# A conv FFN's down product, six of eight tiles by Strassen's scheme, with VectorE making the weight sums

## The reference, cut to what matters

```python
def conv_ffn(x, w_up, conv_w, conv_b, w_down):
    u = causal_depthwise_conv(x @ w_up.astype(x.dtype), conv_w, conv_b)
    g, val = jnp.split(u, [FFN_DIM_2], axis=-1)
    return (jax.nn.gelu(g) * val) @ w_down.astype(x.dtype)
...
        h = h + conv_ffn(rms_norm_2(h, ffn_norm[layer]), ffn_w_up[layer], ffn_conv_w[layer],
                         ffn_conv_b[layer], ffn_w_down[layer])
```

## Time and profile before

| | |
|---|---|
| time, median of 3 runs | 2938.76 us |
| span of the profiled execution, first to last instruction | 2937.1 us |
| mean granted clock of the tensor engine | 0.999 |
| busy: PE, VectorE (DVE), ScalarE (ACT), POOL | 99%, 45%, 44%, 45% |
| up product of the first conv FFN | about 2000 to 2262.6 us |
| down product of the first conv FFN | 2262.6 to 2393.1 us |

### The profile page before, as it was taken

One profiled execution on the slowest core, in us unless ns is written; L12 is line 12 of the kernel. 1 busy time (PEld: TensorE's weight loads), 2 busy tenths in 40 slices (PEclk: granted clock), 3 DMA queues, 4 the chain that ended last, 5 costly groups with the idle time before them and its releaser, 6 DMA issues.

```text
span 2937.1 us, 40238 instructions
## 1 busy us (share of the span) xinstructions
PE 2919.6 (99%) x14312; PEld 2388.5 (81%) x14312; DVE 1309.0 (45%) x2190; ACT 1288.6 (44%) x2017; POOL 1322.3 (45%) x743
## 2 busy tenths in 40 slices
PE   9999999999999999999999999999999999999999
PEld 7888888888878888888888877778888887888887
DVE  5657534221063667434222076654554138455510
ACT  4556545322253556444223265554444228444421
POOL 4454355444434554455444443444444443444443
PEclk9999999999999999999999999999999999999999
DMA  4222232323322232333333322212333322233333
GB/s 145 73 87 80 81 122 92 99 94 100 108 86 87 73 98 68 94 115 106 94 99 101 108 80 71 61 56 94 98 95 98 95 94 94 93 100 93 100 104 90
DMA packets 77275, 273.37 MB, mean 93 GB/s; under 512 B 8776, under 2 KB 9416, under 8 KB 77152
## 3 DMA queue, kind: packets, MB, share of 16 engines
q1 hardware_dynamic: 74112, 266.05, 29.0%
q10 hardware_dynamic: 3040, 5.64, 0.6%
HBM read 269.55 MB, written 2.10 MB: 92 GB/s over the span
## 4 chain that ended last, share of the span: by engine, by line
PE 93%; DVE 2%; ACT 2%; POOL 1%; issue 1%; DMA 0%; SPq 0%; DVEq 0%; ACTq 0%; POOLq 0%
PE ps L822 25%; PE ps L824 25%; PE ps L823 25%; PE ps L1122 2%; PE ps L1153 2%; PE ps L1100 2%; PE ps L1375 2%; PE ps L1381 1%; PE ps L1376 1%; PE ps L1226 1%; PE ps L1232 1%; PE ps L1227 1%; ACT WHI L1534 1%; PE ps L1095 1%; PE ps L1097 0%
## 5 line engine op out<-in xcount | busy, mean ns | idle before, releaser
L2894 POOL TENSOR_TENSOR WLO<-WRAW,WHI 128x1024 fp32r<-128x1024 f32 x393 | 949.8, 2419 | 1158.5 <-ACT WHI L1534 1158.2
L822 PE MATMUL ps<-HH,WHI 128*128 128x512 f32 x2144 | 842.1, 393 | 2.4 <-POOL WLO L2894 0.9
L824 PE MATMUL ps<-HH,WLO 128*128 128x512 f32 x2144 | 834.8, 389 | 0.0
L823 PE MATMUL ps<-HL,WHI 128*128 128x512 f32 x2144 | 834.4, 389 | 0.0
L1534 ACT ACTIVATE WHI<-WRAW 128x1024 fp32r<-128x1024 f32 x467 | 490.6, 1051 | 281.6 <-DMA WRAW<-wall 280.8
L822 PEld LDWEIGHTS ps<-HH,WHI 128*128 128x128 f32 x2144 | 402.5, 188 | 91.2 <-issue 5.3
L824 PEld LDWEIGHTS ps<-HH,WLO 128*128 128x128 f32 x2144 | 402.4, 188 | 84.7
L823 PEld LDWEIGHTS ps<-HL,WHI 128*128 128x128 f32 x2144 | 402.7, 188 | 81.1
L2746 DVE SCALAR_TENSOR_TENSOR ps<-U,COLS,ps 128x512 f32<-128x512 f32 x192 | 145.0, 755 | 122.6 <-ACT ps L1993 108.5
L2228 DVE TENSOR_TENSOR ACC<-ACC,SQ 128x512 f32<-128x512 f32 x78 | 68.4, 877 | 280.5 <-ACT SQ L1819 271.1
L2980 POOL TENSOR_SCALAR SG<-SG,RS 128x512 f32<-128x512 f32 (+3 forms) x104 | 109.9, 1067 | 141.1 <-DVE RS L2508 141.1
(11 more groups left out here) (422 smaller groups left out, 4805.4 us busy)
## 6 DMA issues: line engine op xcount, KB each, us to landing
WRAW<-wall SPq DMA_DIRECT2D x502, 512.0 KB, 3.5
y<-X ACTq DMA_DIRECT2D x8, 256.0 KB, 4.0
X<-xin SPq DMA_DIRECT2D x3, 512.0 KB, 7.9
DFT<-dft ACTq DMA_DIRECT2D x4, 258.0 KB, 4.3
PT_IN<-pin ACTq DMA_DIRECT2D x2, 512.0 KB, 3.7
DIL<-dil ACTq DMA_DIRECT2D x1, 768.0 KB, 4.6
X<-xin SPq DMA_DIRECT2D x2, 256.0 KB, 4.7
COLS<-cols ACTq DMA_DIRECT2D x1, 290.5 KB, 5.3
```

Of the source, the lines that this page charges most:

```text
L822: pe.matmul(out_, WHI[w_at], x_hi, start=first, stop=False)
L823: pe.matmul(out_, WHI[w_at], x_lo, start=False, stop=False)
L824: return pe.matmul(out_, WLO[w_at], x_hi, start=False, stop=last)
L2894: pool.tensor_tensor(WLO[:, s, :], whole, WHI[:, s, :].bitcast(F32), ALU.subtract).then_inc(wt_lo, 1)
```

## The change

The conv FFN is cut into three chunks. A chunk makes 4 rounds of the up product (8 row tiles), then a new stage `down` adds these 8 row tiles' share of all 8 output tiles to X. `down` has 8 units: a direct one (output tile 0, 8 row tiles, as before), six paired ones, and a direct one (output tile 7). Three pairs of output tiles (1 and 2, 3 and 4, 5 and 6) take two paired units each. A paired unit holds two pairs of row tiles for one pair of output tiles, that is, twice four weight blocks of 128 x 128. In place of 8 block products by 256 tokens each it makes 7, of mixed operands (`PRODUCTS`), each by three matmuls of 256 columns: 42 matmuls a unit.

What is new beside the products:
- **weight sums**: four sums of 256 columns a unit, of 2, 2, 3 and 3 blocks, made by VectorE with `tensor_reduce` (`sums_of`). They stand in VectorE's program three units ahead of use, in the up stage before the wait for the unit itself. ScalarE and POOL then split 768 kept columns and 1024 columns of sums (`split_paired`, `remainder_paired`).
- **operand mixes**: at the end of each up round VectorE makes four halves of mixed token columns in three operations (`mixed`), ScalarE copies their high parts, VectorE subtracts for the low.
- **recombination**: per pair ScalarE copies one product and VectorE takes seven operations to add the pair to X (`pair_added`).
- **order on PE**: the last row tile of the first direct unit comes after the first paired unit. The first and third pair use the four convolution banks. The direct tile's slot comes free with the first paired unit's.
- the rounds of both stages are written out; there is no loop. In the first layer's last chunk the work for the next norm follows each finished tile (`finished`).

Cut to its core:

```diff
+CHUNKS = ((0, 4), (4, 4), (8, 4))
+HALF = SEQ // 2
+EXTRA = 4
+A12, A11, A22, A21 = range(4)
+R1, R3, R2, R4 = range(4)
+KEPT = 3 * 2 * P
+PRODUCTS = ((0, "slot", A11, B11), (2, "slot", A12, B21), (1, "extra", R2, T2), (3, "extra", R4, B22),
+            (4, "slot", A22, T4), (5, "extra", R1, T1), (6, "extra", R3, T3))
...
+            def down(st):
+                weights(st.unit(0))
+                pe.wait_ge(bank_free[st.bank(0)], st.use(0))
+                direct(0, 0, range(kt - 1))
+                for j, p, b in paired_steps(st):
+                    if p == 1 and b == 0:
+                        pe.wait_ge(bank_free[st.bank(0)], st.use(4))
...
+                    if p == 2 and b == 0:
+                        pe.wait_ge(S["pair_step"], st.at("pair_step", PAIR_STEPS))
+                    weights(st.unit(j))
...
+                    for i in range(2):
+                        k = 2 * b + i
+                        if p == 0:
+                            pe.wait_ge(S["operand_ready"], up.at("operand_ready", 3, k))
+                        for h, home, block_, x in PRODUCTS:
+                            if p == 0 and k == 0 and h in (0, 4):
+                                pe.wait_ge(S["product_ready"], up.at("product_ready", 1 + h // 4, up.reps - 1))
...
+                            pe.matmul(o, w_hi, FTH[:, row, cols_], start=first, stop=False, skip_group_check=True)
+                            pe.matmul(o, w_hi, FTL[:, row, cols_], start=False, stop=False, skip_group_check=True)
+                            mm = pe.matmul(o, w_lo, FTH[:, row, cols_], start=False, stop=last, skip_group_check=True)
+                    if j == 1:
+                        direct(0, 0, range(kt - 1, kt)).then_inc(unit_used, 2)
+                    else:
+                        mm.then_inc(unit_used, 1)
...
+                direct(j, 3, range(kt)).then_inc(unit_used, 1)
...
+            def split_paired(n):
+                act.activation(WHI[:, s, 0:KEPT], WRAW[:, s, 0:KEPT], ACT.Copy).then_inc(slot_hi, 1)
+                act.wait_ge(*sums_ready(n))
+                act.activation(XHI[:, e, :], XRAW[:, e, :], ACT.Copy).then_inc(wt_hi, 1)
...
-                        t = r * 2 + j // 2
-                        c = t + (FT2 if j % 2 else 0)
+                        c = st.t + r * 2 + j // 2 + (FT2 if j % 2 else 0)
+                        sums_of(st, j, r)
                         dve.wait_ge(unit_used, st.unit(j, r) + 1)
                         scaled(st, j, r, U[:, j, 2:2 + SEQ])
...
-                            remainder(st, (tile_of(t, F2H), tile_of(t, F2L)), SG[:, j, :], 1 + j // 2, r)
-                repeat(dve, st, body)
+                            if j == 3:
+                                mixed(st, r, halves(SG), (2, 3, 6, 7))
+                            remainder(st, (FTH[:, 4 * r + j // 2, :], FTL[:, 4 * r + j // 2, :]), SG[:, j, :], 1 + j // 2, r)
+                    remainder(st, mixed_rows(r), TM[:, :, :], 3, r)
+                repeat(dve, st, body, st.reps)
+
+            def sums_of(st, j, r=0):
+                n = st.unit(j, r) + AHEAD
...
+                w = WRAW[:, s, :].rearrange("p (b c) -> p c b", c=2 * P)
+                dve.wait_ge(raw[s], 16 * (n // SLOTS + 1))
+                for i, blocks in ((R1, slice(A22, A21 + 1)), (R3, slice(A11, A21 + 1, 2)), (R2, slice(A11, A21 + 1)), (R4, slice(A12, A21 + 1))):
+                    dve.tensor_reduce(sum_of(e, i), w[:, :, blocks], AXX, ALU.add).then_inc(summed["vector"], 1)
+
+            def mixed(st, r, b, at):
+                dve.wait_ge(S["product_ready"], st.at("product_ready", 2, r))
+                dve.tensor_tensor(t[:, 0:2, :], b[:, b12:b12 + 1, :].to_broadcast([P, 2, HALF]), b[:, b11:b22 + 1:b22 - b11, :], ALU.subtract)\
+                   .then_inc(S["mixed"], 1)
+                dve.wait_ge(S["mixed"], st.at("mixed", 1, r))
+                dve.tensor_tensor(t[:, 2, :], t[:, 1, :], b[:, b11, :], ALU.subtract).then_inc(S["mixed"], 1)
+                dve.wait_ge(S["mixed"], st.at("mixed", 2, r))
+                dve.tensor_tensor(t[:, 3, :], b[:, b21, :], t[:, 2, :], ALU.add).then_inc(S["mixed"], 1)
...
+            def down(st):
+                for j in range(st.units):
+                    p = ended_at(st, j - 1)
+                    if j == 2:
+                        direct_added(st, 0, 0, 0)
+                    if p is not None:
+                        pair_added(st, p)
+                    sums_of(st, j)
+                    if st.last and j:
+                        for t in tiles_done(st, j - 1):
+                            finished(st, t)
+                direct_added(st, DT - 1, st.units - 1, 3)
...
+            def remainder_paired(n):
...
+                pool.wait_ge(*sums_ready(n))
+                pool.wait_ge(slot_hi, PAIRED[n] + 1)
+                pool.tensor_tensor(WLO[:, s, 0:KEPT], WRAW[:, s, 0:KEPT], WHI[:, s, 0:KEPT].bitcast(F32), ALU.subtract)
+                pool.wait_ge(wt_hi, n + 1)
+                pool.tensor_tensor(XLO[:, e, :], XRAW[:, e, :], XHI[:, e, :].bitcast(F32), ALU.subtract).then_inc(wt_lo, 1)
```

More of the change, by code:

```diff
@@ L124, with pair_order @@
 COL, N_COLS = column_plan()
+def pair_order(pairs, blocks):
+    return [None] + [(p, b) for p in range(pairs) for b in range(blocks)] + [None]
 def unit_list():
@@ L403, in conv_ffn @@
         add("zero_u", per={"zeros_set": 1}, taps=3)
[L404 to L406 removed]
+        for k0, m in CHUNKS:
+            last = 2 * (k0 + m) == FT2
+            up = add("conv_ffn", m, 4, 4, {"conv_begun": 4, "conv_tap_added": 8, "gate_ready": 2, "product_ready": 2, "operand_hi_ready": 3, "operand_ready": 3, "mixed": 3},
+                     l=l, op=op, norm=n if k0 == 0 else None, t=2 * k0)
+            per = {"first_copied": PAIRS, "pair_step": PAIR_STEPS * PAIRS, "direct_added": 2}
+            if last and gain:
+                add("zero", per={"sum_cleared": 1})
+                per |= {"operand_hi_ready": DT, "operand_ready": DT, "square_ready": DT, "square_added": DT}
+            add("down", 1, PAIRS * m // 2 + 2, 8, per, made=up, heads=PAIRS, last=last, gain=gain)
     conv_ffn(0, "rec_norm_20")
@@ L1299, in body @@
                 def body(r):
-                    if isinstance(r, int) and r == 0:
+                    if isinstance(r, int) and r == 0 and st.norm is not None:
                         (opening_fast if st.kind == "conv_ffn" else opening_slow)(st)
@@ new lines, in direct_added, with down @@
+            def direct_added(st, t, j, k):
+                dve.wait_ge(unit_used, st.unit(j) + 1)
+                dve.tensor_tensor(X[:, t, :], X[:, t, :], ps[st.bank(k)][:, :], ALU.add).then_inc(S["direct_added"], 1)
+                dve.engine_nop().then_inc(bank_free[st.bank(k)], 1)
+            def down(st):
+                for j in range(st.units):
+                    p = ended_at(st, j - 1)
+                    if j == 2:
+                        direct_added(st, 0, 0, 0)
+                    if p is not None:
+                        pair_added(st, p)
+                    sums_of(st, j)
+                    if st.last and j:
+                        for t in tiles_done(st, j - 1):
+                            finished(st, t)
+                direct_added(st, DT - 1, st.units - 1, 3)
+                if st.last:
+                    finished(st, DT - 1)
```

174 lines of the change are left out of this document (154 added, 20 removed).

## The result

| | before | after |
|---|---|---|
| time, median (4 runs each on the same chip) | 2938.6 us (2938.32 to 2939.37) | 3012.2 us (3010.39 to 3013.56) |
| ratio, 95% interval | | 1.0249 [1.0235, 1.0264] |
| span of the profiled execution | 2937.1 us | 3011.4 us |
| mean granted clock | 0.999 | 0.990 |

The change costs 73.6 us. The forecast was 2989 us, 50 us slower than before: the direction is right, and the time lies 23 us above it, inside the range.

The account below looks back on a forecast made before the run. PE, busy 99% of the span, was taken to bound the kernel. Matmuls saved (-14.9), stands at six chunk ends (+54.6) and the first layer's last chunk (+10.7) gave +50.4 us, 2989 us; range 2950 to 3040.

Parts of the forecast that it names:

- One sign of being wrong: Among the signs listed against the forecast: waits of PE in the middle of a chunk.
- Part 1, the matmuls: Conv FFN: 256-column matmuls 0.1197 us apart, PE time 123.1 us a layer against 130.6, saving 14.9 us in all.
- Part 2, the price of the sums: VectorE's four weight sums read 512, 512, 768 and 768 elements, 3.0 us a paired unit.
- sums held by POOL: If the sums too stood behind POOL: 18.9 us a chunk, about +115 us; by the port rule they do not.
- The strided read: The sums' strided read is in no row; bounds 1.6 to 5.9 us a unit, 3.0 taken.
- The rival of dearer sums: Sums at 4.4 us a unit, from strided reads or POOL: 16.9 us a chunk, +96, 3035 us; chance 0.14.
- The mixes of a last round: Up rounds: mixing adds 3.4 us against 3.3 of VectorE's slack, 0.6 of it from the first mix behind POOL.
- The first boundary: End of a chunk's up units: PE stands 2.0, 2.5, 1.2 and 3.4 us, 9.1 us a chunk, 54.6 for six.
- The clock: Clock drops to 1.2 GHz for one pair unit at each boundary: +5.0 x 6 on top, 3019 us; chance 0.08.
- The first layer's last chunk: The next norm's work can stand behind POOL, so PE stands 3.0, 2.3 and 5.4 us: 10.7 us.
- Faster: Direct tile and first pair units cover VectorE's backlog, under 2.5 us a chunk: -7.7, 2931 us; chance 0.10.

Follow-up runs that it names:

- Experiment 2: The changed kernel with the fourth weight sum reading three blocks instead of four (block A12 left out): 2986.5 us.
- experiment 4: The changed kernel with matmuls of a constant, written to a free bank, put into the two long stands of each chunk: 3012.8 us.
- experiment 11: The changed kernel with the norm's work on finished tiles in the first layer's last chunk done on 64 of 512 columns: 3006.4 us.

## Why the prediction was right, and what was mis-sized

**Right in mechanism.** Once a chunk PE stands for VectorE and POOL, and that outweighs the matmuls saved; the boundaries are read off one engine's order. One sign of being wrong showed faintly: of the five chunks without the norm's work, four have a wait in their middle, 0.2 to 0.8 us before the sixth paired unit.

**Where the 23 us lie.** The forecast has 6.6 us a chunk (54.6 less 14.9, over six), and the period is 10.0 above the 130.6 of before: 20 us over six chunks. The other 3 lie outside: the first conv FFN starts 2.05 us later than before, behind stages that the change leaves alone (in the other kernels it starts from 1.0 earlier to 2.4 later), and the recurrent block behind it takes 1.0 more.

**Part 1, the matmuls: right.** Spacing 0.12 as forecast (212 of the 251 steps from one short matmul to the next in the first chunk's down stage are 0.11 to 0.12, and 33 are the 0.21 to 0.22 of the slow stretches). With no sums the period is 129.1 against 128.1 worked out. The saving of 14.9 us is there and is spent.

**Part 2, the price of the sums: the step that failed.** "The four sums of a pair unit read 512, 512, 768 and 768": the fourth reads 1024. The reductions of two blocks came as forecast (0.70), of three 1.03 for 0.95, and the fourth 1.97 for 0.95: 4.2 us a unit for 3.0. Experiment 2 takes that one difference away and finds 2986.5 us, 2.5 from the forecast: this term carries the error. (A smaller slip: the prediction has about +115 us for sums held by POOL, at 18.9 us a chunk; its own steps give 18.9 x 6 - 14.9 + 10.7, +109.) The strided read, which the range had feared, costs the two-block form nothing.

**The rival of dearer sums** happened as to the price (4.2 against its 4.4) and not as to the time: 3012 for its 3035. The boundary has more slack than my steps gave it. The gap of VectorE between copy and first tap is 0.85 us where the earlier trace rows show 1.10, and the taps take 1.55 for 1.66; over four up units that is over a microsecond that VectorE is less late. The mixes of a last round lost 2.1 us to POOL, but in the second of them, after the product.

**The first boundary**, stand by stand. Forecast: 2.0 before the first paired unit, 2.5 before its later products, 1.2 before the direct tile's last row, 3.4 before the third paired unit. Measured: 1.41, 2.52, none, 3.91, and 0.56 before the sixth, where I had none. The third paired unit came late for another reason than mine: I had its sums and their low part; it was the direct tile's bank, which VectorE hands back after adding that tile, and I had not costed that addition, which stands in VectorE's order behind the sums of two units. With sums near 3.0 us (experiment 2) the list is the forecast's own: 0.45, 1.61, 0.71 (FTL, the direct tile's last row) and 3.19 (XLO). Those are 6.0 us where I had 9.1, and the half clock and the moments around the stands fill the 8.4 us a chunk which that kernel loses (136.5 less 128.1). So its nearness to the forecast is in part one error against another.

**The clock: a rival that occurred and cost nothing by itself.** The rival had it at 1.2 GHz for a unit a boundary, +5.0 us; in the first chunk it fell twice, for about 16 matmuls each, 3.0 us, and experiment 4 gives that back without a gain.

**The first layer's last chunk**: stands of 3.0, 2.3 and 5.4 forecast; 0.49, 3.49 and 3.06 measured, 7.0 us for 10.7. As a whole this chunk is 10.7 us longer than the one before it (151.6 for 141.0, from its first up matmul to the next stage), just the forecast; 7.7 of that are stands, and part of the rest is slow matmuls after them. So the sum is right and its parts are not, which is in part luck. The mechanism (two-input operations ahead of a recombination, behind POOL) is borne out by experiment 11. The sixth unit's stand of 3.49 also holds the dearer sums.

**Faster** was given 0.10. It needed a loss under 2.5 us a chunk, which only the kernel with no sums has, and that one is even with the kernel before: its period is only 1.5 us under the 130.6, and 6.3 of the six chunks' 9 us go in the first layer's last chunk. My price for this rival (-7.7) left that out.

## What to carry to other kernels

Where one engine runs in order and makes operands for later units, cost each boundary as a list of what stands ahead of the instruction that the bound engine waits for; small instructions that hand back a buffer belong in that list. Read the operand shape of every new operation out of the slice itself, element by element: here one block too few was a third of the loss. Before moving work to another engine, compare that engine's time per unit with the bound engine's: GpSimd needs 7.3 us a unit against 5.0, and the kernel with all six units' sums there is 35 us slower than the one with two.

## What the runs showed of the hardware that was not expected

- A reduction of VectorE over strided blocks: 0.70 us for 512 elements read, 1.03 for 768, and 1.97 for 1024, with 256 results each. The two forms of 512, over neighbouring blocks and over every other block, are alike (0.63 to 0.72). The step from three to four blocks (0.94) is nearly three times that from two to three (0.33). Why is open; no run here keeps the elements read and changes the group length or the layout.
- An operation of VectorE with two SBUF inputs that meets a running operation of POOL ends a short time after it, and that time goes with its own width: 0.09 us for 64 columns, 0.28 for 256, 0.55 for 512. So 64 columns took 2.43 us where 512 had taken 2.90.
- After stands of 3.9 to 4.5 us the tensor engine ran 12 to 27 matmuls of 256 columns at 0.21 us instead of 0.12 (1.2 instead of 2.4 GHz), and after those of 2.5 us 12 to 16 in five chunks and none in the fourth, so that the length of the stand alone does not tell; right after the stands of 1.4 us there were none. Filled stands kept the clock at 1.00, and the time stayed.
